# Moving the weight halves and the moving operands by 16 to 96 bytes in SBUF, in a two-block transformer kernel

## The chip, the cores and the metric

The kernel runs on one core of a Trainium2 chip. The metric is the device time of one execution in microseconds: the median of several runs.

## What is computed

Two different transformer blocks are applied in turn to 256 tokens of width 2048 in float32: a retention and state-space mixer with a gated output and a feed-forward layer, then a mixer of attention, gated linear attention and a short convolution, and a second feed-forward layer. Cut to the products that take the time:

```python
# first block
proj = h @ w_in                                        # 2048 -> 13312 columns
y_ret = (silu(g_ret) * ret) @ w_ret_out
glu_a, glu_b = split(y_ssm @ w_s5_glu, 2)
y = (sigmoid(gate_r) * y_ret + sigmoid(gate_s) * y_s5) @ w_out
a, b = split(h @ w_ffn_in, 2); y = (silu(a) * b) @ w_ffn_out     # width 5632
# second block: its own w_in, three branch products, w_out, gate/up/down of 5632
```

All of it is dense float32 work on weights that are read once, about 700 MB in all.

## The kernel before

The output features lie on partitions: each output block of 128 features is a sum over input blocks of 128 (the index `k`), with a 128 x 128 weight tile as the stationary operand and the 256 tokens as the moving one.

**The split.** A float32 product is made of several products in the reduced type `float32r`. Each weight block of 16 tiles (1 MB) comes by DMA into one of four ring slots, `ring_raw`. ScalarE writes its rounded half to `ring_hi` (`split_hi`, L1017), and VectorE writes the remainder, raw minus rounded, to `ring_lo` (`split_lo`, L1477). `ring_raw` and `ring_lo` of a slot share one address, so this subtraction is in place. The activations are held split too: in `h_split`, `ffn_split`, `mixed_split` and the like, each `k` has 256 rounded columns and behind them 256 remainder columns.

**The products.** `products()` makes one tile's work. In the first block's mixer (`p.thirds`) it is three matmuls of 256 columns: rounded weights by rounded activations (L635), rounded weights by remainders (L636), remainder weights by rounded activations (L637). Everywhere else it is two: rounded weights by all 512 columns (L638), then remainder weights by 256 (L639). Each matmul has its own weight load, which the profile shows as PEld. The order of all work is written out by hand; SyncE's queue issues the weight DMAs as slots come free, ScalarE rounds, VectorE subtracts, TensorE waits for `lo_done` of a block and then runs its 16 tiles.

**The addresses.** All operands lie at fixed SBUF addresses. The allocator is a stack: a tensor starts behind the one before it, rounded up to 32 bytes, and what is opened in a closed `ExitStack` gives its place to the next. The first ring slot starts at byte 1152 of each partition, which is 9 x 128. Worked out from the declared sizes, these are the starts as remainders of 128 bytes. Every step inside a tensor that a matmul makes (512 bytes from tile to tile, 1024 and 2048 in the moving operand) is a multiple of 128, so the remainder holds for each matmul of that tensor.

| operand | role | before | after |
|---|---|---|---|
| `ring_hi` (all slots) | weights, rounded half | 0 | 0 |
| `ring_raw`, `ring_lo` | weights, raw and remainder half | 0 | 16 |
| `h_split`, `ffn1_split`, `ffn2_split` | moving | 32 | 32 |
| `o_att_split`, `o_gla_split`, `y_conv_split` | moving | 32 | 32 |
| `ret_split`, `merged_split` | moving | 64 | 32 |
| `y_ssm_split` | moving | 64 | 96 |
| `mixed_split` | moving | 0 | 96 |

Of the kernel before, what the change touches and what calls it, by code (L numbers as in the profile page):

```python
# [23 lines left out]
F32R = mybir.dt.float32r  # L24
# [5 lines left out]
P = 128  # L30
T = 256
D = 2048
KT = D // P
# [18 lines left out]
PI_IN = 3.1415925  # L52
ROUND = 1.5 * 2.0 ** 23
SLOTS = 4
W, ADA = "w", "ada"


class Phase:
# [7 lines left out]
    def __init__(self, iters, blocks, outs, summed=False, beside=1):  # L66
# [5 lines left out]
        self.asides = len(blocks) - len(self.tiles)  # L72
        assert len(self.tiles) % SLOTS == 0 and outs % 2 == 0
        self.offsets = [sum(n for _, n in blocks[:j]) * P * P for j in range(len(blocks))]
# [8 lines left out]
    def uses(self, g, m):  # L83

        return g * (len(self.tiles) // SLOTS) + (self.first_block // SLOTS + m // SLOTS + 1)

# [116 lines left out]
def program(nc, dram, out):  # L203
    stored, ph = schedule(), stages()
    with ExitStack() as ctx:
        def sb(stack, name, shape, dt=F32):
            return stack.enter_context(nc.sbuf_tensor(name, shape, dt))

        def sem(name):
            return ctx.enter_context(nc.semaphore(name))  # L210


        raw, hi, lo = [], [], []
        for s in range(SLOTS):
            with ExitStack() as shared:
                raw.append(sb(shared, f"ring_raw{s}", [P, KT, P]))
            lo.append(sb(ctx, f"ring_lo{s}", [P, KT, P], F32R))
            hi.append(sb(ctx, f"ring_hi{s}", [P, KT, P], F32R))
        with ExitStack() as shared:
            s5_tab = [sb(shared, f"s5_tab{i}", [P, 2, 2, T]) for i in range(2)]  # L220
# [25 lines left out]
        with ExitStack() as block1:  # L246
            c_act = sb(block1, "c_act", [P, D])
            with ExitStack() as mixer:
                log_g = sb(mixer, "log_g_sb", [P, HEADS])
                wv = [[], []]  # L250
                with ExitStack() as shared:
                    wv[0] = [sb(shared, f"wv_a{n}", [P, 4, 4, P]) for n in range(4)]
# [4 lines left out]
                with ExitStack() as shared:  # L257
                    first_gates = sb(shared, "first_gates", [P, 4, 2 * T])
                merged = sb(mixer, "merged_split", [P, KT, 2 * T], F32R)
                with ExitStack() as shared:  # L260
                    sb(shared, "y_ssm_first", [P, HALF // 2, 2 * T])
                    aside_y = sb(shared, "aside_y", [P, D])
# [56 lines left out]
        with ExitStack() as block2:  # L319
            with ExitStack() as mixer:  # L320
# [27 lines left out]
                    a_end = sb(early, "a_end", [P, GLA_HEADS, T])  # L348
                t0 = sb(mixer, "merge0", [P, KT, T])
                conv_w = sb(mixer, "conv_w_sb", [P, HALF, 3])  # L350
                with ExitStack() as early:
                    gq = sb(early, "gq", [P, T])
                    gk = sb(early, "gk", [P, T])
                    gv_t = sb(early, "gv_t", [P, 2, T])
                    gr_t = sb(early, "gr_t", [P, 2, T])
                    gr_act = sb(early, "gr_act", [P, 2, T])
                    q_in = [sb(early, f"q_in{i}", [P, T]) for i in range(2)]
                    k_in = sb(early, "k_in", [P, T])
                    k_dec = sb(early, "k_dec", [P, T])
                    gv_n = sb(early, "gv_n", [P, 2, T])  # L360
                    k_dec_n = sb(early, "k_dec_n", [P, 3, P])
                    intra = sb(early, "intra", [P, 2, P])
                    state = [sb(early, f"state{i}", [P, T]) for i in range(3)]
                    go = sb(early, "go", [P, 2, T])
                    go_sq = sb(early, "go_sq", [P, 2, T])
                    go_std = sb(early, "go_std", [P, T])
                    go_rstd = sb(early, "go_rstd", [P, T])
                    att_q = [sb(early, f"att_q{i}", [P, T]) for i in range(2)]
                    att_k = [sb(early, f"att_k{i}", [P, T]) for i in range(2)]
                    att_v = [sb(early, f"att_v{i}", [P, T]) for i in range(2)]  # L370
# [27 lines left out]

        raw_in = [sem(f"raw_in{s}") for s in range(SLOTS)]
        wv_in = [[sem(f"wv_in{b}{part}") for part in range(2)] for b in range(2)]  # L400
        x_first = [sem(f"x_first{n}") for n in range(2)]
        c_set, hf_done, v_step, v_done, v_evac = (sem(n) for n in ("c_set", "hf_done", "v_step", "v_done", "v_evac"))
        late_row_in, late_row_free = sem("late_row_in"), sem("late_row_free")
        slot_free = [sem(f"slot_free{s}") for s in range(SLOTS)]
        hi_done, lo_done = sem("hi_done"), sem("lo_done")
# [103 lines left out]
        def _(sp):  # L509
# [40 lines left out]
            def weight(p, g, m, src):  # L550

                sp.wait_ge(slot_free[m % SLOTS], p.uses(g, m) - 1)
                sp.dma_start(raw[m % SLOTS][:].rearrange("p k c -> p (k c)"), src).then_inc(raw_in[m % SLOTS], 16)
# [1842 lines left out]
```

## Time and profile before

| | |
|---|---|
| median of 3 runs | 3386.57 us (3383.78 to 3386.83) |
| the profiled execution's own time | 3381.64 us |
| its span, first to last instruction | 3379.9 us |
| TensorE matmul busy | 3307.3 us, 98% of the span, 20368 matmuls |
| VectorE busy | 2324.5 us, 69% |
| ScalarE busy | 1452.4 us, 43% |
| mean granted TensorE clock | 0.992 |
| DMA | 706 MB, 209 GB/s |

How to read it: an engine's busy time is the union of its instructions; matmuls are pipelined, so one matmul's duration reaches over the start of the next, and what a matmul costs in a stream is the distance from its start to the start of the next. Durations and these distances move together here: the profile gives the 256-column matmul of `merged_split` 276 ns and starts the next about 113 ns later; it gives that of `ffn_split` 282 ns and the next starts about 118 ns later.

### The profile page before, as it was taken

How to read it: one execution, taken by the hardware profiler on the slowest of the kernel's cores; microseconds unless marked ns; L12 is line 12 of the kernel's file. 1: busy time of each engine (PE TensorE's matmuls, PEld its weight loads, DVE VectorE, ACT ScalarE, POOL GpSimd, SP SyncE). 2: the span in 40 equal slices, each digit the busy share in tenths (PEclk: the TensorE clock that was granted, in tenths of full speed). 3: DMA queues.
4: the chain of work that ended last, by engine and by line, in shares of the span. 5: the costliest groups of instructions: out<-in, count | busy, mean ns of one | idle time of the engine just before them, and what ended most of it. 6: DMA issues, size and time to landing. Idle time of an engine off the chain costs nothing.

```text
span 3379.9 us, 51972 instructions
## 1 busy us (share of the span) xinstructions
PE 3307.3 (98%) x20368; PEld 2937.2 (87%) x20368; DVE 2324.5 (69%) x2503; ACT 1452.4 (43%) x1464; POOL 435.2 (13%) x309
## 2 busy tenths in 40 slices
PE   6999999999899999999899999999999999999998
PEld 3599999999788888888788888888888888888887
DVE  6789979877766666666666667566767766666554
ACT  2256664444443444433454443444344444344332
POOL 1047668500100000000000000000003000000000
PEclk9999999999999999999999999999999999999999
DMA  9885456678545555577534444555555555555554
GB/s 378 349 328 180 180 202 237 251 292 311 198 175 188 192 191 186 195 268 254 198 137 169 167 162 178 193 183 186 192 186 196 188 188 186 189 192 186 185 191 149
DMA packets 119746, 706.34 MB, mean 209 GB/s; under 512 B 13776, under 2 KB 28752, under 8 KB 41312
## 3 DMA queue, kind: packets, MB, share of 16 engines
q1 hardware_dynamic: 109280, 695.96, 56.2%
q10 hardware_dynamic: 10368, 9.02, 0.8%
q8 instruction: 68, 1.11, 0.1%
q14 instruction: 30, 0.25, 0.0%
HBM read 702.83 MB, written 2.10 MB: 209 GB/s over the span
## 4 chain that ended last, share of the span: by engine, by line
PE 90%; DVE 5%; ACT 1%; DMA 1%; SPq 1%; issue 1%; DVEq 0%; ACTq 0%
PE acc L638 45%; PE acc L639 24%; PE acc L635 6%; PE acc L636 6%; PE acc L637 6%; DVE ring_raw L1499 1%; DVE ring_lo L1477 1%; DMA ring_raw<-w_ada 1%; SPq L542 1%; PE p_y L705 1%; PE p_norm L687 1%; PE p_z L715 1%; ACT ring_hi L1017 0%; DMA ring_raw<-w_out 0%; DVE rstd L1524 0%
## 5 line engine op out<-in xcount | busy, mean ns | idle before, releaser
L638 PE MATMUL acc<-h_split,ring_hi 128*128 128x512 f32 x4736 | 1655.9, 392 | 9.5 <-DVE h_split L1539 4.5
L1477 DVE TENSOR_TENSOR ring_lo<-ring_raw,ring_hi 128x2048 fp32r<-128x2048 f32 (+2 forms) x560 | 1265.1, 2260 | 550.2 <-ACT ring_hi L1017 549.1
L639 PE MATMUL acc<-h_split,ring_lo 128*128 128x256 f32 x4736 | 1337.6, 282 | 0.0
L1017 ACT ACTIVATE ring_hi<-ring_raw 128x2048 fp32r<-128x2048 f32 (+2 forms) x560 | 1040.0, 1862 | 458.6 <-DMA ring_raw<-w_down 150.4
L638 PEld LDWEIGHTS acc<-h_split,ring_hi 128*128 128x128 f32 x4736 | 891.9, 188 | 197.6 <-issue 10.0
L639 PEld LDWEIGHTS acc<-h_split,ring_lo 128*128 128x128 f32 x4736 | 897.9, 190 | 0.4
L638 PE MATMUL acc<-ffn_split,ring_hi 128*128 128x512 f32 x1408 | 488.2, 390 | 0.0
L2146 POOL TENSOR_TENSOR sq_sum<-sq_sum,tile 128x256 f32<-128x256 f32 x60 | 79.6, 1326 | 2561.6 <-ACT tile L1043 2561.6
L639 PE MATMUL acc<-ffn_split,ring_lo 128*128 128x256 f32 x1408 | 397.1, 282 | 0.0
L635 PE MATMUL acc<-h_split,ring_hi 128*128 128x256 f32 x1152 | 329.2, 286 | 0.3 <-ACT val_a L1030 0.2
L637 PE MATMUL acc<-h_split,ring_lo 128*128 128x256 f32 x1152 | 321.6, 279 | 0.0
L636 PE MATMUL acc<-h_split,ring_hi 128*128 128x256 f32 x1152 | 321.6, 279 | 0.0
L638 PEld LDWEIGHTS acc<-ffn_split,ring_hi 128*128 128x128 f32 x1408 | 264.4, 188 | 55.4
L639 PEld LDWEIGHTS acc<-ffn_split,ring_lo 128*128 128x128 f32 x1408 | 266.1, 189 | 0.0
L635 PEld LDWEIGHTS acc<-h_split,ring_hi 128*128 128x128 f32 x1152 | 216.6, 188 | 1.8 <-issue 0.6
L636 PEld LDWEIGHTS acc<-h_split,ring_hi 128*128 128x128 f32 x1152 | 216.6, 188 | 1.1 <-issue 0.2
L637 PEld LDWEIGHTS acc<-h_split,ring_lo 128*128 128x128 f32 x1152 | 216.6, 188 | 0.0
L1310 ACT ACTIVATE ffn_split<-ffn_a 128x256 f32 (+1 forms) x88 | 36.8, 418 | 361.5 <-DVE ffn_a L1903 361.5
L1492 DVE TENSOR_REDUCE ffn_b<-acc 128x256 f32<-128x512 f32 x88 | 60.8, 691 | 143.2 <-PE acc L639 143.2
L1043 ACT ACTIVATE tile<-x_res 128x256 f32 (+1 forms) x80 | 33.1, 417 | 152.1 <-DVE x_res L2127 85.2
L1308 ACT ACTIVATE ffn_t<-ffn_a 128x256 f32<-128x256 f32 x88 | 36.7, 417 | 129.3 <-DVE ffn_a L1899 119.2
L2204 POOL TENSOR_TENSOR s_x<-s_w,s_tab 128x512 f32<-128x512 f32 x32 | 86.6, 2707 | 29.9 <-DVE s_w L1688 29.8
(381 smaller groups left out, 3936.5 us busy)
## 6 DMA issues: line engine op xcount, KB each, us to landing
ring_raw<-w_ff SPq DMA_DIRECT2D x88, 1024.0 KB, 4.8
ring_raw<-w_down SPq DMA_DIRECT2D x64, 1024.0 KB, 4.8
ring_raw<-w_ffb SPq DMA_DIRECT2D x56, 1024.0 KB, 4.8
ring_raw<-w_mix SPq DMA_DIRECT2D x48, 1024.0 KB, 4.8
ring_raw<-w_ada SPq DMA_DIRECT2D x32, 1024.0 KB, 11.9
ring_raw<-w_heads SPq DMA_DIRECT2D x32, 1024.0 KB, 4.8
ring_raw<-w_ret SPq DMA_DIRECT2D x32, 1024.0 KB, 5.2
ring_raw<-w_glu SPq DMA_DIRECT2D x32, 1024.0 KB, 4.9
```

The lines of the kernel that those rows point to most:

```text
L635: mm(dst[:, 0:T], hi[s][:, t, :], moving[:, k, 0:T], start=start, stop=False)
L636: mm(dst[:, 0:T], hi[s][:, t, :], moving[:, k, T:], start=False, stop=False)
L637: return mm(dst[:, 0:T], lo[s][:, t, :], moving[:, k, 0:T], start=False, stop=stop)
L638: mm(dst[:], hi[s][:, t, :], moving[:, k, :], start=start, stop=False, skip_group_check=True)
L639: return mm(dst[:, T:], lo[s][:, t, :], moving[:, k, 0:T], start=False, stop=stop, skip_group_check=True)
L1017: run(hi[s][:, 0:n, :], raw[s][:, 0:n, :], COPY).then_inc(hi_done, 1)
L1308: run(t[i % 2][:], a[i % 2][:], ACT.Tanh, scale=0.5).then_inc(f_tanh, 1)
L1310: run(dst[:, 4 * g + (first + i), 0:T], a[i % 2][:], COPY, scale=0.5).then_inc(f_hi, 1)
L1477: tt(lo[s][:, 0:n, :], raw[s][:, 0:n, :], hi[s][:, 0:n, :], SUB).then_inc(lo_done, 1)
L1492: v.tensor_reduce(dst, acc[o % 2][:].rearrange("p (c t) -> p t c", c=2), AX_X, ADD).then_inc(sum_done, 1)
L2146: tt(sq_sum[:], sq_sum[:], tile[b][:], ALU.add).then_inc(sq_used, 1)
L2204: tt(xs[:], w[:], sin, ALU.mult)
```

## The change

The allocations alone are changed; no instruction, order or size of a transfer is. Each `ring_raw` and `ring_lo` gets 128 bytes more per partition, and its 16 tiles are taken from the fifth float on, that is 16 bytes past the tensor's start. Three unused pads (96, 64 and 96 bytes) are put ahead of `ret_split` and `merged_split`, of `y_ssm_split` and of `mixed_split`. The table above has what comes out for the operands of the large matmuls. Everything behind the ring moves up by 512 bytes, and some of the mixer's small tensors, the state-space matrices among them, change their remainder by 32.

```diff
+LO_AT = slice(4, 4 + KT * P)
...
             with ExitStack() as shared:
-                raw.append(sb(shared, f"ring_raw{s}", [P, KT, P]))
-            lo.append(sb(ctx, f"ring_lo{s}", [P, KT, P], F32R))
+                raw.append(sb(shared, f"ring_raw{s}", [P, KT * P + 32])[:, LO_AT].rearrange("p (k c) -> p k c", k=KT))
+            lo.append(sb(ctx, f"ring_lo{s}", [P, KT * P + 32], F32R)[:, LO_AT].rearrange("p (k c) -> p k c", k=KT))
             hi.append(sb(ctx, f"ring_hi{s}", [P, KT, P], F32R))
...
                 log_g = sb(mixer, "log_g_sb", [P, HEADS])
+                sb(mixer, "ret_step", [P, 24])
...
                 merged = sb(mixer, "merged_split", [P, KT, 2 * T], F32R)
+                sb(mixer, "y_step", [P, 16])
...
                 conv_w = sb(mixer, "conv_w_sb", [P, HALF, 3])
+                sb(mixer, "mixed_step", [P, 24])
```

## Rows read from the trace of the kernel before

**Rows 1.** The page: busy time of each engine (share of the span) and instructions.

```profile
PE 3307.3 (98%) x20368; PEld 2937.2 (87%) x20368; DVE 2324.5 (69%) x2503; ACT 1452.4 (43%) x1464; POOL 435.2 (13%) x309
```

**Rows 2.** The page: the chain that ended last, by engine and line.

```profile
PE 90%; DVE 5%; ACT 1%; DMA 1%; SPq 1%; issue 1%; DVEq 0%; ACTq 0%
PE acc L638 45%; PE acc L639 24%; PE acc L635 6%; PE acc L636 6%; PE acc L637 6%; DVE ring_raw L1499 1%; DVE ring_lo L1477 1%; DMA ring_raw<-w_ada 1%; SPq L542 1%; PE p_y L705 1%; PE p_norm L687 1%; PE p_z L715 1%; ACT ring_hi L1017 0%; DMA ring_raw<-w_out 0%; DVE rstd L1524 0%
```

**Rows 3.** Groups of instructions: shape, count, busy us, mean ns, idle before.

```profile
L638 PE MATMUL acc<-h_split,ring_hi 128*128 128x512 f32 x4736 | 1655.9, 392 | 9.5 <-DVE h_split L1539 4.5 <-DVE h_split L1537 4.4 <-DVE ffn_a L1492 0.4
...
L1477 DVE TENSOR_TENSOR ring_lo<-ring_raw,ring_hi 128x2048 fp32r<-128x2048 f32 (+2 forms) x560 | 1265.1, 2260 | 550.2 <-ACT ring_hi L1017 549.1
L1017 ACT ACTIVATE ring_hi<-ring_raw 128x2048 fp32r<-128x2048 f32 (+2 forms) x560 | 1040.0, 1862 | 458.6 <-DMA ring_raw<-w_down 150.4 <-DMA ring_raw<-w_mix 64.7 <-DMA ring_raw<-w_ret 49.8
...
L638 PE MATMUL acc<-mixed_split,ring_hi 128*128 128x512 f32 x256 | 89.9, 393 | 0.0
```

**Rows 4.** Matmuls by moving tile: duration ns min/median/max, first and last start.

```profile
L638 PE MATMUL acc<-ffn_split,ring_hi x1408: 390/390/390, 1417.9 to 3365.1; 128*128 128x512 f32 x176
L639 PE MATMUL acc<-ffn_split,ring_lo x1408: 282/282/282, 1418.1 to 3365.3; 128*128 128x256 f32 x176
...
L638 PE MATMUL acc<-y_conv_split,ring_hi x128: 390/390/390, 2248.6 to 2542.2; 128*128 128x512 f32 x128
...
L638 PE MATMUL acc<-mixed_split,ring_hi x256: 387/396/400, 2542.5 to 2632.0; 128*128 128x512 f32 x128
L639 PE MATMUL acc<-mixed_split,ring_lo x256: 278/283/285, 2542.8 to 2632.3; 128*128 128x256 f32 x128
...
L636 PE MATMUL acc<-h_split,ring_hi x1152: 277/280/284, 154.6 to 808.7; 128*128 128x256 f32 x192
...
L636 PE MATMUL acc<-ret_split,ring_hi x256: 276/280/283, 450.7 to 633.6; 128*128 128x256 f32 x128
...
L636 PE MATMUL acc<-y_ssm_split,ring_hi x256: 276/276/283, 658.1 to 814.1; 128*128 128x256 f32 x128
...
L636 PE MATMUL acc<-merged_split,ring_hi x256: 276/276/276, 814.4 to 902.8; 128*128 128x256 f32 x128
```

**Rows 5.** Timeline of TensorE, start us and us: first and last of nine pairs.

```profile
1500.08 0.39 PE L638 MATMUL acc<-ffn_split,ring_hi 128*128 128x512 f32 x1
1500.31 0.28 PE L639 MATMUL acc<-ffn_split,ring_lo 128*128 128x256 f32 x1
...
1503.20 0.39 PE L638 MATMUL acc<-ffn_split,ring_hi 128*128 128x512 f32 x1
```

**Rows 6.** Timeline, `mixed_split`: a short pair, and the start six pairs later.

```profile
2580.08 0.39 PE L638 MATMUL acc<-mixed_split,ring_hi 128*128 128x512 f32 x1
2580.30 0.28 PE L639 MATMUL acc<-mixed_split,ring_lo 128*128 128x256 f32 x1
...
2582.18 0.39 PE L638 MATMUL acc<-mixed_split,ring_hi 128*128 128x512 f32 x1
```

**Rows 7.** Timeline, three-matmul stages: `merged_split` (17 on), then `h_split` (14 on).

```profile
860.04 0.28 PE L637 MATMUL acc<-merged_split,ring_lo 128*128 128x256 f32 x1
...
861.97 0.28 PE L636 MATMUL acc<-merged_split,ring_hi 128*128 128x256 f32 x1
...
199.81 0.28 PE L636 MATMUL acc<-h_split,ring_hi 128*128 128x256 f32 x1
...
201.45 0.28 PE L635 MATMUL acc<-h_split,ring_hi 128*128 128x256 f32 x1
```

**Rows 8.** Windows: busy us of each engine (instructions), PEclk, DMA share, GB/s.

```profile
0.00:100.00 100.00, 73.89 (x166) 33.56 (x167) 66.08 (x113) 23.35 (x45) 16.82 (x21) 0.93 0.99 384
...
200.00:300.00 100.00, 99.64 (x793) 97.56 (x793) 95.60 (x122) 58.88 (x62) 72.62 (x47) 1.00 0.63 231
...
1000.00:1100.00 100.00, 100.00 (x579) 88.63 (x578) 63.73 (x63) 41.45 (x37) 0.00 (x0) 1.00 0.53 190
```

**Rows 9.** DMA issues: tile, count, KB each, median us to landing.

```profile
ring_raw<-w_ff SPq DMA_DIRECT2D x88, 1024.0 KB, 4.8
...
aside_z<-w_heads SPq DMA_DIRECT2D x9, 1024.0 KB, 4.9
```

**Rows 10.** Plain float32 matmuls of 256 columns: duration ns min/median/max.

```profile
L705 PE MATMUL p_y<-s_x,s_c_sb x128: 377/378/382, 230.1 to 652.2; 128*128 128x256 f32 x128
```

## The prediction

> **What bounds the kernel.** I read the page first: TensorE is busy in 98% of the span and no other engine above 69% [rows 1]. The chain of the work that ended last says the same by line: 90% of it is TensorE, and the five matmul lines of `products()` carry 87% [rows 2]. So time goes one for one with the distance between matmul starts, as long as TensorE stays fed. The windows show that: from 1000 us on a stretch of 100 us has TensorE busy for all of it and VectorE for 64 [rows 8].
>
> Then I asked what a matmul costs in the stream. In the second feed-forward product nine pairs (L638 and L639) take from 1500.08 to 1503.20 us, 3.12 us, or 346.7 ns a pair: 228 ns for the one of 512 columns and 118 for the one of 256 [rows 5]. Their durations differ by 390 - 282 = 108 ns for 256 columns [rows 4], 0.42 ns a column, which is the cycle of the clock's upper level of 2.4 GHz (the granted clock is 1.00 from 1000 to 1100 us too [rows 8]). 768 columns are then 320 ns, and 26.7 ns of each pair are something else.
>
> The reader is to see next that this rest is not one fixed price. The same instructions, with the same shapes and with the same ring, have other durations by moving tensor [rows 4], and the tensors differ in their start address. With `merged_split` (64 past a 128-byte line) every matmul of 256 columns has 276 ns; with `ffn_split` (32 past) its neighbour in a pair has 282; with `h_split` in the three-matmul stages (32 past) 277 to 284, median 280. With `mixed_split` (0 past) the 512-column one swings between 387 and 400, where all of 32 past have 390 without spread. In starts: 17 matmuls of `merged_split` in 1.93 us are 113.5 ns each, 14 of `h_split` in 1.64 us are 117.1 [rows 7]; `mixed_split` takes 2.10 us for six pairs, 350 ns a pair [rows 6]. A duration less 163 ns is the distance to the next start in all of these. But the address is not all of it: `ret_split`, at 64 like `merged_split`, goes from 276 to 283 with median 280, and `y_ssm_split`, at 64 too, has a median of 276 with a tail to 283 [rows 4]. One pair of addresses can thus run in more than one pattern.
>
> **The change part by part.** No instruction and no wait is added or removed. There are 4736 + 1408 + 3 x 128 = 6528 pairs (the three tensors of 128 have one pattern, that of `y_conv_split`) whose moving operand stays at 32 and whose remainder weights go from 0 to 16; 256 pairs of `mixed_split`, from 0 to 96; and 1152 + 3 x 256 = 1920 groups of three, of which 1152 (`h_split`) keep their moving address [rows 3, 4].
>
> *The pairs.* The weight load of the remainder half starts with the 512-column matmul and is read beside it; that of the next rounded half is read beside the 256-column matmul. The change alters the first combination of addresses directly and the second by where in its pattern it begins. No row has weights at 16, so the cost is bounded by what the rows show at other remainders. The lowest are 387 ns for 512 columns (2580.08 to 2580.30 is one such [rows 6]) and 276 for 256 columns [rows 4]. Against 390 and 282 that is 3 + 6 = 9 ns a pair, 6528 x 9 = 58.8 us. Lower still would be the fixed part of `merged_split`, 113.5 - 106.7 = 6.8 ns, on both: 220.1 + 113.5 = 333.6 ns a pair, 13.1 less than now, 85.5 us. Above stands the pair of `mixed_split`, 393 + 283 in the means against 390 + 282, 4 ns more, 26 us. I take 58.8: it is the lowest that rows show for both shapes, and an address that serves both weight halves is more likely near what `merged_split` has than at a new low. The reason for the sign is that 26.7 ns of a pair are now lost to something that the rows show to depend on addresses, and that the present combination loses more in its 256-column member (11.6 ns over 106.7) than `merged_split` does in each of three.
>
> *`mixed_split`.* 393 and 283 in the mean to 387 and 276: 13 ns x 256 = 3.3 us. In the worst case it stays.
>
> *The groups of three.* `h_split` from 117.1 to 113.5 ns: 3.6 x 3456 = 12.4 us. `ret_split` from a median of 280 to 276, 4 x 768 = 3.1. `y_ssm_split` and `merged_split` have nothing to give. From 200 to 300 us, though, VectorE is busy for 95.6 of 100 [rows 8]: there a faster TensorE waits for `lo_done` instead. I keep half of 15.5, 7.8 us. In the bad case `y_ssm_split` and `merged_split`, 1536 matmuls, lose 4 ns each, 6.1 us.
>
> *Who feeds the pairs.* A block of 16 pairs takes 5.55 us now and 5.40 then. Its subtraction takes 2.26 us on VectorE and its rounding 1.86 on ScalarE [rows 3], 63.7 and 41.5 of 100 busy with all else [rows 8], and its transfer 4.8 us to landing, of four in flight [rows 9]. If the 16 bytes made one of them 5% slower, cover would hide it. Below nothing I see no reason for a gain there.
>
> *The DMA writes.* All rows of 8 KB now begin 16 bytes past a line. A tensor at 64 past lands as one at 0 past: 4.9 us for `aside_z`, 4.8 for `ring_raw` [rows 9]. 16 past no row shows. It matters where DMA sets the pace, in the first 150 us, with a DMA share of 0.99 in the first 100 [rows 8]. One further line of 128 bytes per row would be 1/64, 2.3 us of these 150; the other bound is 0. I take 0, since the 64-past row differs by 0.1 us in 4.8 at most, and keep 2.3 for the range.
>
> *The small products.* L705 and its kind (plain float32) have 378 ns, 215 to the next start, for 256 columns at half the rate, 213 ns [rows 10]: 2 ns of rest. There is next to nothing in them to win.
>
> Sum: 58.8 + 3.3 + 7.8 = 69.9 us. The profiled execution's own time is 3381.64 (span 3379.9 and 1.7 around it); less 69.9 it is 3311.7. The median of the runs is 4.9 above that execution, so I forecast 3316.6 us on the scale of the median.
>
> **A page that speaks against it.** The rows say that the distance of like matmuls depends on the moving tensor's place. The Trainium skill, "TensorE: Matmul & The Clock Gate", section "Step-by-step: what each phase is for", says that TensorE reads moving and stationary operands through two SBUF ports of their own, so that loading the next weights takes no read bandwidth from the running matmul. By that rule the addresses of the weights would be free, and the change would give nothing, 3387. This case's trace does not agree in full, since 276 and 282 ns [rows 4] have the same weights at the same address, but it doesn't show that it is the weights' address that counts.
>
> **The rivals.**
> - *Only a part is given back*, chance 0.22. The remainder load is read beside the 512-column matmul alone. If just that one goes from 390 to 387, it is 3 x 6528 = 19.6 us; if just the 256-column one, 6 x 6528 = 39.2. With or without the 11 us of the rest, 3336 to 3367, middle 3352. For it: only one of two weight addresses moves in 6528 pairs. Against: the two are locked in one pattern, 390 and 282 without spread, and so change together.
> - *Nothing changes*, chance 0.12: the weights' address doesn't matter, only the moving one's. Then the pairs stay, `mixed_split` gains up to 3, and `merged_split` and `y_ssm_split` lose up to 6: 3384 to 3390. For it: rows differ only by moving tensor, all with the ring at 0. Against: `ret_split` and `merged_split` differ at one moving address, so something beside it takes part.
> - *Slower*, chance 0.21: at 16, the remainder weights fall into a pattern as `mixed_split`'s. It is one mechanism, the pair of weight load and 512-column matmul, at 4 ns more: 26 us, and 6 more where `merged_split` leaves its good address, 3413 to 3419. It decides as soon as a pair takes over 348 ns (1 ns x 6784 = 6.8 us is the measurement's bound). For it: the only other combination seen in pairs is worse than the present one on average. Against: within it stand pairs of 387, lower than the present.
> - *Deeper*, chance 0.05: pairs at 333.6 ns or below, 3281 or lower (85.5, 16.4 x 256 = 4.2 for `mixed_split` and all 15.5 of the groups of three are 105.2 us). If the rest of each matmul were 2 ns as in the plain products [rows 10], a pair would be 324 ns, 154 us less over all pairs: 3222 with the groups' 11.
>
> **How the numbers follow.** The forecast, pairs between 333 and 340 ns (3281 to 3325), has 0.40. Faster by over 0.2% are the forecast, the partial and the deeper case: 0.67. Within 0.2%, about what a measurement of this kernel can tell from no change: 0.12. Slower: 0.21. The likeliest case's own range is 3281 to 3325. For 8 in 10 it reaches over the partial and the unchanged case and takes in the 2.3 us of DMA, to 3396, which leaves out most of the slower case, and below to 3272, which leaves out most of the deeper one.
>
> **What would show it.** In the profile after: `ffn_split` at L638 with 387 or less and at L639 with 276; 9 pairs in 3.04 us in place of 3.12; about 593 matmuls per 100 us for 579; `merged_split` still at 276 at its new address; L1477 and L1017 with 2260 and 1862 ns; `ring_raw` landing in 4.8 us. Wrong would be the forecast if 390 and 282 stand as they are, if a spread as `mixed_split`'s appears in all pairs, or if TensorE begins to wait for `ring_lo`.

## The result and the profile after

The changed kernel takes 3400.58 us (median of 5, 3399.07 to 3402.09); the kernel before 3386.57 in the same comparison. The ratio is 1.0044, 95% interval 1.0032 to 1.0057: slower by 0.4%, where the prediction named 3316.6 and a faster time. The ratios here, though not the medians, leave out two single executions of later versions, one of 8797.62 us in twelve (80/16) and one of 11486.07 in ten (48/112), which nothing here explains. The changed kernel's profiled execution took 3399.39 us, with a span of 3397.6. Lines are four further down than before: L642 and L643 are the pair, L639 to L641 the group of three.

The page's first part and the shares of the chain:

```profile
PE 3326.8 (98%) x20368; PEld 2933.9 (86%) x20368; DVE 2323.0 (68%) x2503; ACT 1452.1 (43%) x1464; POOL 429.4 (13%) x309
...
PE 93%; DVE 4%; ACT 1%; DMA 1%; SPq 1%; issue 0%; DVEq 0%; ACTq 0%
PE acc L642 46%; PE acc L643 23%; PE acc L639 6%; PE acc L640 6%; PE acc L641 6%; DVE ring_raw L1503 1%; DMA ring_raw<-w_ada 1%; SPq L546 1%; PE p_z L719 1%; PE p_y L709 1%; DVE ring_lo L1481 1%; PE p_norm L691 0%; DVE rstd L1528 0%; ACT ring_hi L1021 0%; ACT tile L1047 0%
```

TensorE is busy for 3326.8 us in place of 3307.3 [rows 1], 19.5 more, with the same 20368 matmuls; VectorE and ScalarE have what they had. The feeders are untouched by the 16 bytes (groups of instructions: count, busy us, mean ns; then the DMA issues):

```profile
L1481 DVE TENSOR_TENSOR ring_lo<-ring_raw,ring_hi 128x2048 fp32r<-128x2048 f32 (+2 forms) x560 | 1263.4, 2257 | 557.9 <-ACT ring_hi L1021 556.8
L1021 ACT ACTIVATE ring_hi<-ring_raw 128x2048 fp32r<-128x2048 f32 (+2 forms) x560 | 1040.0, 1861 | 460.5 <-DMA ring_raw<-w_down 152.5 <-DMA ring_raw<-w_mix 66.3 <-DMA ring_raw<-w_ret 50.1
```

```profile
ring_raw<-w_ff SPq DMA_DIRECT2D x88, 1024.0 KB, 4.8
```

So the time is in the distances between matmuls. By moving tile, duration ns min/median/max:

```profile
L642 PE MATMUL acc<-ffn_split,ring_hi x1408: 389/393/403, 1426.6 to 3382.8; 128*128 128x512 f32 x176
L643 PE MATMUL acc<-ffn_split,ring_lo x1408: 277/280/284, 1426.8 to 3383.1; 128*128 128x256 f32 x176
...
L642 PE MATMUL acc<-mixed_split,ring_hi x256: 389/392/447, 2557.4 to 2646.5; 128*128 128x512 f32 x128
...
L640 PE MATMUL acc<-merged_split,ring_hi x256: 277/281/284, 818.6 to 909.0; 128*128 128x256 f32 x128
```

Before, `ffn_split` had 390 and 282 without any spread, and `merged_split` 276 [rows 4]. Now the pair wanders, and how is the clue. These are starts of L643 that lie 16 pairs, one ring slot's worth, apart (timeline of TensorE, first in a gate and up stage of the first block, then in the second block's):

```profile
1000.05 0.28 PE L643 MATMUL acc<-h_split,ring_lo 128*128 128x256 f32 x1
...
1005.66 0.28 PE L643 MATMUL acc<-h_split,ring_lo 128*128 128x256 f32 x1
...
1011.26 0.28 PE L643 MATMUL acc<-h_split,ring_lo 128*128 128x256 f32 x1
...
1016.81 0.28 PE L643 MATMUL acc<-h_split,ring_lo 128*128 128x256 f32 x1
...
1022.38 0.28 PE L643 MATMUL acc<-h_split,ring_lo 128*128 128x256 f32 x1
...
2800.18 0.28 PE L643 MATMUL acc<-h_split,ring_lo 128*128 128x256 f32 x1
...
2805.76 0.28 PE L643 MATMUL acc<-h_split,ring_lo 128*128 128x256 f32 x1
...
2811.30 0.28 PE L643 MATMUL acc<-h_split,ring_lo 128*128 128x256 f32 x1
```

In the first stretch it is 5.61, 5.60, 5.55 and 5.57 us, and then the same four again; worked out from the exact starts, 351.2, 349.9, 346.4 and 348.4 ns a pair. In the second it is 5.58 and 5.55 us, 348.8 and 346.6 ns a pair, and then these two again. Four is the number of slots, and two is after how many slots the addresses repeat within 256 bytes, as the experiments show. Before the change all four slots had 346.7. From 1000 to 1300 us there are 1721 matmuls where there were 1733, 349.0 ns a pair.

Summed over all distances from a matmul to the next, `h_split` has 11.4 us more than before, `ffn_split` 3.9, `merged_split` 2.2, `y_ssm_split` 2.2, the three tensors of 128 pairs 0.7; `mixed_split` has 0.4 less, `ret_split` 0.4 less, everything else 1.5 less. That is 18.1; the first matmul starts 0.4 us earlier, and the span has 17.7 more. The 11.4 us of `h_split` are two things: 8.1 in its pairs, and 3.4 in its groups of three, which go from 350.3 to 353.4 ns in the mean. All pairs whose moving operand stays where it was lose 12.6 us together, 1.9 ns each.

### The profile page after: what moved, and what is told of

It is laid out like the page before. It is cut to its first block, busy times and chain, and to the rows that moved or that the text cites. A ratio compares the mean times of both kernels' runs of the same rounds, so it can differ in the third digit from the quotient of the medians.

```text
span 3397.6 us, 51972 instructions
## 1 busy us (share of the span) xinstructions
PE 3326.8 (98%) x20368; PEld 2933.9 (86%) x20368; DVE 2323.0 (68%) x2503; ACT 1452.1 (43%) x1464; POOL 429.4 (13%) x309
## 4 chain that ended last, share of the span: by engine, by line
PE 93%; DVE 4%; ACT 1%; DMA 1%; SPq 1%; issue 0%; DVEq 0%; ACTq 0%
PE acc L642 46%; PE acc L643 23%; PE acc L639 6%; PE acc L640 6%; PE acc L641 6%; DVE ring_raw L1503 1%; DMA ring_raw<-w_ada 1%; SPq L546 1%; PE p_z L719 1%; PE p_y L709 1%; DVE ring_lo L1481 1%; PE p_norm L691 0%; DVE rstd L1528 0%; ACT ring_hi L1021 0%; ACT tile L1047 0%
## 5 line engine op out<-in xcount | busy, mean ns | idle before, releaser
L642 PE MATMUL acc<-h_split,ring_hi 128*128 128x512 f32 x4736 | 1665.4, 396 | 9.4 <-DVE h_split L1543 4.5
L1481 DVE TENSOR_TENSOR ring_lo<-ring_raw,ring_hi 128x2048 fp32r<-128x2048 f32 (+2 forms) x560 | 1263.4, 2257 | 557.9 <-ACT ring_hi L1021 556.8
L643 PE MATMUL acc<-h_split,ring_lo 128*128 128x256 f32 x4736 | 1327.0, 280 | 0.0
L1021 ACT ACTIVATE ring_hi<-ring_raw 128x2048 fp32r<-128x2048 f32 (+2 forms) x560 | 1040.0, 1861 | 460.5 <-DMA ring_raw<-w_down 152.5
L642 PEld LDWEIGHTS acc<-h_split,ring_hi 128*128 128x128 f32 x4736 | 894.1, 189 | 215.1 <-issue 10.2
L643 PEld LDWEIGHTS acc<-h_split,ring_lo 128*128 128x128 f32 x4736 | 894.5, 189 | 0.4
L642 PE MATMUL acc<-ffn_split,ring_hi 128*128 128x512 f32 x1408 | 492.1, 394 | 0.0
L643 PE MATMUL acc<-ffn_split,ring_lo 128*128 128x256 f32 x1408 | 394.2, 280 | 0.0
L639 PE MATMUL acc<-h_split,ring_hi 128*128 128x256 f32 x1152 | 330.6, 287 | 0.3
L641 PE MATMUL acc<-h_split,ring_lo 128*128 128x256 f32 x1152 | 322.7, 280 | 0.0
L642 PEld LDWEIGHTS acc<-ffn_split,ring_hi 128*128 128x128 f32 x1408 | 264.6, 188 | 61.4
L643 PEld LDWEIGHTS acc<-ffn_split,ring_lo 128*128 128x128 f32 x1408 | 265.4, 189 | 0.0
L639 PEld LDWEIGHTS acc<-h_split,ring_hi 128*128 128x128 f32 x1152 | 216.9, 188 | 1.7 <-issue 0.6
L641 PEld LDWEIGHTS acc<-h_split,ring_lo 128*128 128x128 f32 x1152 | 217.1, 188 | 0.0
```

The lines of the kernel that those rows point to most:

```text
L639: mm(dst[:, 0:T], hi[s][:, t, :], moving[:, k, 0:T], start=start, stop=False)
L641: return mm(dst[:, 0:T], lo[s][:, t, :], moving[:, k, 0:T], start=False, stop=stop)
L642: mm(dst[:], hi[s][:, t, :], moving[:, k, :], start=start, stop=False, skip_group_check=True)
L643: return mm(dst[:, T:], lo[s][:, t, :], moving[:, k, 0:T], start=False, stop=stop, skip_group_check=True)
L1021: run(hi[s][:, 0:n, :], raw[s][:, 0:n, :], COPY).then_inc(hi_done, 1)
L1481: tt(lo[s][:, 0:n, :], raw[s][:, 0:n, :], hi[s][:, 0:n, :], SUB).then_inc(lo_done, 1)
```

## The experiments

Theory A was: the 16 bytes of the remainder halves spoil the pattern. Theory B: the ring tensors have grown by 128 bytes each, so that one slot is 16512 bytes from the next in place of 16384; if the chip's cycle of addresses is longer than 128 bytes, the slots are no longer alike. Theory C was that the traffic of other engines causes the lost time. A combination of addresses is written as remainder weights/moving operand, in bytes past the rounded weights within 256 bytes; 80/16 is one. Values in ns per pair or per group of three are worked out from the starts in the trace; a pair is one matmul of 512 columns and one of 256.

**Only the slots' distance.** The change's ring with `LO_AT` from 0, no pads:

```diff
+LO_AT = slice(0, KT * P)
-                raw.append(sb(shared, f"ring_raw{s}", [P, KT, P]))
+                raw.append(sb(shared, f"ring_raw{s}", [P, KT * P + 32])[:, LO_AT]...)
...  (ring_lo the same)
```

> Ring slots get the 128 bytes more, but raw and remainder halves stay on the 128-byte line, and there are no pads: only the distance of the slots in memory changes, 16512 bytes for 16384. Theory A (the 16 bytes cost the time): as before, 3387 within 5 us, pairs of ffn_split at 390 and 282 without spread. Theory B (the slots' distance costs it): pairs change from slot to slot, 390 is spread, and the time moves by more than 5 us.

Measured: 3402.98 us, ratio 1.0056 (1.0039 to 1.0073). The remainder halves stand on the 128-byte line and the loss is there in full. But the edit changes two things at once. The slots differ in the moving operand's distance (160 in one, 32 in the next), and in all of them the remainder halves stand 128 bytes further from the rounded ones. No whole kernel takes these apart; the sweep below has 350.0 ns for 128/160 and 346.7 for 128/32. By moving tile:

```profile
L639 PE MATMUL acc<-ffn_split,ring_hi x1408: 391/394/400, 1427.4 to 3386.8; 128*128 128x512 f32 x176
```

**The ring's part of the change, no pads.** The diff of the change without its three `sb(mixer, ...)` lines.

> The ring's part of the change (16 bytes and 128 more per tensor) without the three pads. Theory A and B alike: the large pairs are as in the changed kernel, so about 3400 less what the pads cost: merged_split and y_ssm_split keep 64 bytes past the line. If the pads are what made the groups of three slower (4 ns x 1536 = 6 us), this one has 3394; if not, 3400.

Measured: 3401.88 us, 1.0055 (1.0038 to 1.0072). The pads are not what made it slow.

**The 16 bytes without the other distance.** The tensors grow by 256 bytes:

```diff
+LO_AT = slice(4, 4 + KT * P)
+                raw.append(sb(shared, f"ring_raw{s}", [P, KT * P + 64])[:, LO_AT]...)
...  (ring_lo the same)
```

> The 16 bytes of the change, but the tensors grow by 256 bytes in place of 128, so that all four slots are alike within 256 bytes; no pads. Theory B (the slots' distance did the harm, not the 16 bytes): the sweep has 346.7 ns for remainder weights 16 and moving 32 past the rounded ones, so 3386 within 6 us and one pair time in all slots. Theory A (the 16 bytes harm): 3395 or more.

Measured: 3389.79 us, 1.0017 (1.0007 to 1.0026), with 1733 matmuls from 1000 to 1300 us and 346.7 ns a pair in all slots. The 16 bytes cost the pairs nothing. The 0.17% is in the groups of three: those of `merged_split` go from 340.0 to 353.3 ns, those of `y_ssm_split` from 344.2 to 353.1, those of `h_split` from 350.3 to 352.5. By moving tile:

```profile
L637 PE MATMUL acc<-merged_split,ring_hi x256: 277/278/283, 820.5 to 911.2; 128*128 128x256 f32 x128
```

**The pads alone.** Only the three `sb(mixer, ...)` lines.

> The three pads alone, the ring as before. The pads move mixed_split from 128 to 224 past the rounded weights within 256 bytes (the sweep: 351.1 and 353.3 ns a pair, +0.6 us over 256 pairs), ret_split and merged_split from 64 to 160, y_ssm_split from 64 to 224: against now 340 to 353 ns a group the sweep has 356.0 and 355.0. Expected is 3 to 10 us slower than before, 3389 to 3396; if the pads do nothing, 3386.

Measured: 3387.21 us, 1.0010 (1.0000 to 1.0019): 0 to 0.2% slower, 2.5 us in the medians, just below the 3 to 10 that were expected.

**Address sweeps.** A kernel in which TensorE alone streams pairs, or groups of three, from chosen addresses; the rest of the computation is left out. Its core:

```python
for h, l, m in COMBOS:
    for n in range(STEPS):
        wh = hi[:, h // 4 + t * P:h // 4 + t * P + P]      # rounded weights at h bytes
        wl = lo[:, l // 4 + t * P:l // 4 + t * P + P]      # remainder weights at l
        at = m // 4 + t * 2 * T                            # moving operand at m
        mm(acc[:], wh, mv[:, at:at + 2 * T], ...)
        mm(acc[:, T:], wl, mv[:, at:at + T], ...)
```

> Leaves out all of the reference's computation (it copies x to the output) and streams pairs of matmuls, 512 and 256 columns, 24 pairs for each of 16 x 20 combinations of the remainder weights' and the moving operand's start, the rounded weights at 0 of a 512-byte line, all other engines idle. Theory A, only the remainder of 128 bytes counts: combinations that differ by 128 or 256 bytes have the same ns per pair; remainder weights at 0 with moving at 32 give 346.7 as in the kernel before. Theory B, the cycle of addresses is longer than 128 bytes, so that the four slots, which now stand 128 bytes apart in it, are four different cases: 0 and 128 differ by ns. Theory C, the other engines' traffic causes the lost time: all combinations have one and the same time, below 346.7.

> The same sweep with groups of three matmuls of 256 columns, 16 groups for each combination; it too leaves out all of the reference's computation. Theory A: 113.3 ns per matmul with both weights at 0 and moving at 64, 116.7 with moving at 32, and the same 128 bytes further. Theory B: other values 128 bytes further. Theory C: one value everywhere.

Some cells of the sweep of pairs, the rounded weights at 0 (ns per pair, the last 12 of 24):

```
remainder \ moving    0     32     64     96    128    160    256    288    320
      0             353.3  346.7  348.9  350.0  351.1  346.7  353.3  346.7  353.3
     64             346.7  353.3  340.0  346.7  346.7  353.3  346.7  348.9  340.0
    128             346.7  346.7  346.7  350.0  352.9  350.0  350.0  346.7  346.6
    256             353.3  346.7  348.9  350.0  351.1  346.7  353.3  346.7  353.3
    320             346.7  353.3  340.0  346.7  346.7  353.3  346.7  348.9  340.0
```

Moving the remainder weights by 256 bytes leaves 99 of 100 cells as they are (99 of 100 for groups of three), by 128 bytes only 57 of 160. For the remainder weights the cycle is 256 bytes. Moving the moving operand by 256 leaves 102 of 128, by 128 only 50 of 192: 256 is much nearer to a cycle for it than 128, but it is not shown to be one. Of the 26 cells that change, 18 are combinations that have one value from both starts in the full grid below, so a second pattern that a stream can fall into, or a longer cycle of the moving operand, are both open. No sweep moves the rounded weights alone. With nothing else running, remainder weights at 0 and moving at 32 give the kernel's own pattern, and at 128 that of `mixed_split`, member by member (by tile of the sweep; `aa` is 0, `ac` 32, `ai` 128, `ae` 64):

```profile
L66 PE MATMUL at_aa_aa_ac<-moving,w_hi x24: 390/390/396, 33.8 to 41.7; 128*128 128x512 f32 x24
L67 PE MATMUL at_aa_aa_ac<-moving,w_lo x24: 279/282/282, 34.0 to 42.0; 128*128 128x256 f32 x24
...
L66 PE MATMUL at_aa_aa_ai<-moving,w_hi x24: 387/396/402, 84.2 to 92.3; 128*128 128x512 f32 x24
...
L66 PE MATMUL at_aa_ae_ae<-moving,w_hi x24: 389/389/393, 721.7 to 729.5; 128*128 128x512 f32 x24
L67 PE MATMUL at_aa_ae_ae<-moving,w_lo x24: 276/276/278, 721.9 to 729.7; 128*128 128x256 f32 x24
```

390 and 282, and 387/396, are the figures of [rows 4]. That refutes theory C, and theory A in its form with 128 bytes.

**The full grid, twice.** All 256 combinations in steps of 16, each behind one matmul of another length (ns per pair, the last 8 of 16), and then some of them with all three operands moved together.

> Leaves out the reference's computation like the first sweep. Every combination of remainder weights and moving operand in steps of 16 bytes over 256, twice, each behind one matmul of another length, and then 128 combinations with the rounded weights at 16, 64, 128 and 208 of 256. Theory B2, only the distances between the three operands within 256 bytes count: the third part repeats the first at equal distances, and the second repeats the first. Theory B3, the state in which a stream begins counts too: some combinations have two values, in the first and the second part, while a few (remainder weights and moving both 64 past the rounded ones, 340.0 in six of six cases of the first sweep) keep one. Theory B4, absolute addresses count: the third part differs from the first for most combinations.

Times go from 340.0 to 363.4 ns, mean 349.3. In 200 of 256 combinations both starts give one value; in 56 they don't, so a stream can settle in more than one pattern. Five combinations have 340.0 from both starts: 32/144, 48/112, 80/16, 208/64 and 208/112 (remainder weights/moving operand past the rounded weights). With the rounded weights at 64 or 128 the single-valued cells repeat in 17 and 15 of 21, at 16 or 208 in 7 and 6 of 21. I passed over that second finding and built two versions of the kernel on distances alone.

**Two versions of the whole kernel at such distances.** Rounded halves 16 bytes into their tensors, slots 16640 bytes apart, pads for the moving operands:

```diff
+HI_AT = slice(4, 4 + KT * P)
-            hi.append(sb(ctx, f"ring_hi{s}", [P, KT, P], F32R))
+            hi.append(sb(ctx, f"ring_hi{s}", [P, KT * P + 24], F32R)[:, HI_AT]...)   # 80/16; raw and lo + 40
+        sb(ctx, "h_step", [P, 40])
+                sb(mixer, "ret_step", [P, 16])
+                sb(mixer, "mixed_step", [P, 40])
...  (48/112: raw and lo + 48, hi + 16, h_step 8, mixed_step 40, no ret_step)
```

> The whole kernel, with remainder weights 80 and the moving operands of all pairs 16 past the rounded weights within 256 bytes, the same in all four slots. The theory (only the three operands' distances within 256 bytes set the time of a matmul in the stream): the sweeps have 340.0 ns in three of three cases, so 6528 pairs x 6.7 = 43.5 us less, mixed_split 2.8 less, the groups of three of h_split at 353.1 for 350, 3.6 us more, merged_split and y_ssm_split (now 112 past) 5 more: 3347, within 10. The rival, that other engines' traffic or the starts of the blocks throw the stream out of the good pattern: pairs between 343 and 350, and 3365 to 3400.

> The same with remainder weights 48 and moving operands 112 past the rounded weights, the other combination that the sweeps have at 340.0 in three of three. The theory: groups of three of h_split at 354.7 ns, 5.4 us more, else as the one before: 3349 within 10. The rival: 3365 to 3400.

Measured: 3387.90 us, 1.0010 (1.0001 to 1.0019), and 3393.28, 1.0023 (1.0014 to 1.0033). Both missed: the pairs have 346.7 ns, the first with members of 392 and 279, the second with 394 and 278, where the sweeps had 340.0, with 389 and 276 for 80/16 and 388 and 275 for 48/112.

**Groups of three, the full grid.**

> Leaves out the reference's computation. The full sweep in steps of 16 bytes for groups of three matmuls of 256 columns, twice. The theory of distances within 256 bytes and of more than one pattern for some of them: a few combinations have 340.0 ns a group in both parts, many have two values, and those of the first sweep of groups come out again. If instead groups of three have one value for each combination, the spread between merged_split and ret_split needs another cause.

Six combinations have 340.0 in both parts and many have two values: 210 of 256 have one. Remainder weights 0 and moving 64, which is `merged_split` before, had 353.4 in both parts here, and 340 (276 a member) in the kernel.

**What held the two versions back?** One kernel with eight segments.

> Leaves out the reference's computation. Six combinations of remainder weights and moving operand (0 and 32, 16 and 32, 48 and 112, 80 and 16, 64 and 64, 208 and 64 past the rounded weights), 64 pairs each, in eight segments: alone; with the moving operand 90 KB up; with the weights far up; in a hardware loop with two banks; beside VectorE subtractions; beside ScalarE copies; beside 1 MB transfers; beside all three. The full kernels had 346.7 ns for 48 and 112 and for 80 and 16, the sweeps 340.0. Theory D, distance in memory beyond 256 bytes counts: the segment with the moving operand or the weights far up has 346.7 for them. Theory E, the loop or the change of banks counts: only the loop's segment has it. Theory F, the traffic of another engine moves the stream into its other pattern: 340.0 in the quiet segments and 346.7 beside one of the three, which names the engine.

Theories D, E and F all fell. 80/16 has 340.0 in every segment, with 19.7 of 20 us of VectorE or ScalarE beside it or 216 GB/s of transfers. Two windows (each begins in 80/16 and ends in 64/64, which has 340.0 too), and the tile alone (`near`) and beside all three (`byall`):

```profile
783.00:803.00 20.00, 20.00 (x120) 17.67 (x119) 0.00 (x0) 19.68 (x11) 0.00 (x0) 1.00 0.00 1
...
1050.00:1070.00 20.00, 20.00 (x120) 17.67 (x119) 19.73 (x9) 19.68 (x11) 0.00 (x0) 1.00 0.63 215
```

```profile
L90 PE MATMUL near_af_ab<-moving,w_hi x64: 387/389/399, 99.3 to 120.8; 128*128 128x512 f32 x64
```

```profile
L90 PE MATMUL byall_af_ab<-moving_far,w_hi x64: 388/389/399, 1034.5 to 1056.0; 128*128 128x512 f32 x64
```

48/112 had 356.7 in all quiet segments and 340.0 in the sweeps: again two patterns of one combination.

**The place of all three.** Eight combinations of distances, six of them in the table, the rounded weights at 0, 16, ... 128, three starts.

> Leaves out the reference's computation. Eight pairs of distances, each with the rounded weights at 0, 16, ... 128 past a line of 256 bytes, from three starts, 32 pairs each. Theory G, beside the distances the place of the three operands within 64 bytes counts (in the sweep the third part at 64 and 128 repeated the first, at 16 and 208 it did not, and these two agreed): values repeat when all three operands are moved by 64 bytes and not when by 16; the distances 80 and 16 with the rounded weights at 48 have 346.7 with members of 229 and 117, 48 and 112 with them at 80 has 346.7 with 232 and 115, as in the full kernels. Theory H, only the distances count and the full kernels were held in another pattern by something else: 340.0 for 80 and 16 at every place.

Values against the place of the rounded weights, counted over 15 streams (multiples of 32) and 12 streams (16 more than one), rounded ns:

```
remainder/moving   on a multiple of 32         16 past one
   0/32            347 in 15                   353 in 10, 347 in 2
  48/112           340 in 12, 357 in 3         347 in 12
  80/16            340 in 14, 353 in 1         347 in 12
  64/64            340 in 11, 350 in 4         350 in 12
 208/64            351 in 13, 340 in 2         340 in 12
 208/112           340 in 13, 353 in 2         351 in 7, 353 in 5
```

So the place within 32 bytes counts, not within the 64 of theory G. In the two versions the rounded weights stood at 48 and 80, 16 past a multiple of 32; the sweep has for these places what they had, with the same members (rounded weights at 48 with 80/16, then at 208/64 with them at 0 and at 16):

```profile
L67 PE MATMUL at_ad_ai_ae<-moving,w_hi x32: 392/392/437, 1332.5 to 1343.3; 128*128 128x512 f32 x32
L68 PE MATMUL at_ad_ai_ae<-moving,w_lo x32: 277/279/279, 1332.8 to 1343.6; 128*128 128x256 f32 x32
...
L67 PE MATMUL at_aa_an_ae<-moving,w_hi x32: 393/394/450, 1835.2 to 1846.2; 128*128 128x512 f32 x32
...
L67 PE MATMUL at_ab_ao_af<-moving,w_hi x32: 388/388/429, 1869.3 to 1879.9; 128*128 128x512 f32 x32
```

**Two versions with the rounded weights on a multiple of 32**, chosen before that sweep was read. `LO_AT` begins at float 52 or 16, the tensors grow by 64 floats, `h_step` is of 8 floats, `ret_step` of 48 or 8, `mixed_step` of 40:

> The full kernel with the rounded weights at 128, remainder weights 208 and moving operands of the pairs 64 past them, thus at places within 64 bytes that the sweeps had, and with 340.0 in ten of ten cases; the operands of the groups of three other than h_split 32 past. Theory G: 340.0 ns a pair, 43.5 us less, mixed_split 2.8 less, groups of three 7 more: 3347 within 10. Theory H: 346.7 a pair and 3385 to 3395.

> The same with remainder weights and moving operands 64 past, the other operands of three at 128 past. The sweeps have 340.0 in eight of nine cases and 350.0 in one. Theory G: 340.0 and 3348 if every stream falls into the better pattern, 350.0 and 3413 if into the other, and between them if both occur. Theory H: as for the one before.

Measured: 3413.98 us, 1.0090 (1.0076 to 1.0105), and 3359.76, 0.9935 (0.9913 to 0.9958). The first was expected fast and is the slowest of all: ten streams had 340.0 there, and the sweep by places, not yet read, has 351 in 13 of 15, in all three with the rounded weights at 0, where the sweeps before it had theirs, so the value hangs on something beside the addresses that no run names; the kernel has 350.9 to 351.4. The second beats both kernels, with runs from 3348.68 to 3378.11: in the trace most of its `h_split` pairs and all of `ffn_split` stand at 340.0, and the branch products and `mixed_split` of the second block at 350.0, the two values of 64/64. By moving tile:

```profile
L642 PE MATMUL acc<-ffn_split,ring_hi x1408: 389/389/389, 1414.3 to 3341.2; 128*128 128x512 f32 x176
...
L642 PE MATMUL acc<-mixed_split,ring_hi x256: 395/395/395, 2532.8 to 2622.0; 128*128 128x512 f32 x128
```

**A version with one pattern.** 208/64 with the rounded weights at 176 of 256, 16 past a multiple of 32; all moving operands of pairs taken 16 bytes into their tensors:

```diff
+        def stepped(stack, name, k, dt=F32):
+            t = sb(stack, name, [P, k * 2 * T + 8], dt)
+            return t[:, 4:4 + k * 2 * T].rearrange("p (k c) -> p k c", k=k)
...
+            hi.append(sb(ctx, f"ring_hi{s}", [P, KT * P + 56], F32R)[:, HI_AT]...)   # from float 4; raw and lo + 8
+        sb(ctx, "h_step", [P, 16])
+        h = stepped(ctx, "h_split", KT, F32R)
...  (normed, ffn1_split, ffn2_split, o_att and o_gla in one tensor, y_conv_split, mixed_split the same, with pads of 56, 56, 56, 56 and 32 floats)
```

> The full kernel at the distances 208 and 64 again, but with the rounded weights 16 past a multiple of 32 (176 of 256), the moving operands of all pairs at 240 and the remainder weights at 128. The sweep by places has 340.0 ns in 12 of 12 cases there, and 350.9 or 340.0 with the rounded weights on a multiple of 32, which was the version at 3414. Distances within 256 bytes and the place within 32 bytes fix the pair: 340.0 in every stretch, 6528 x 6.7 = 43.5 us less, mixed_split 2.8 less, groups of three unknown, between 20 less and 12 more: 3330 to 3355, and runs within 5 us of each other, for there is one pattern. If something else of the kernel counts: 346.7 or more, 3385 and above.

Measured: 3348.12 us, runs from 3347.82 to 3348.48, ratio 0.9896 (0.9879 to 0.9912): 1.0% faster than the kernel before and, from the two ratios, 1.5% than the changed one, and inside the window that was named. The pairs give back what was expected; the groups of three take back about 11 us of it (an estimate from the trace: 354.8 ns for 350.3 in `h_split`, 353.3 for 340.0 in `merged_split`, 353.5 for 344.2 in `y_ssm_split`). By moving tile, and ten pairs in 3.40 us:

```profile
L650 PE MATMUL acc<-ffn_split,ring_hi x1408: 388/388/389, 1417.1 to 3331.8; 128*128 128x512 f32 x176
L651 PE MATMUL acc<-ffn_split,ring_lo x1408: 275/275/275, 1417.3 to 3332.0; 128*128 128x256 f32 x176
```

```profile
1500.08 0.39 PE L650 MATMUL acc<-ffn_split,ring_hi 128*128 128x512 f32 x1
...
1503.48 0.39 PE L650 MATMUL acc<-ffn_split,ring_hi 128*128 128x512 f32 x1
```

**The groups of three, 16 bytes further.**

> Leaves out the reference's computation. The full sweep of groups of three with all three operands 16 bytes further. If the place within 32 bytes counts, the groups' times differ from those of the full sweep before in many cells; if distances alone count for groups of three, they repeat it.

Of the 170 combinations with one value in each of the two grids, 47 have the same in both. The place counts for them as well.

## Why the prediction was wrong

**What bounds the kernel: right.** Every version's time followed the distance of its matmuls; VectorE's busy time stayed between 2323 and 2329 us and ScalarE's between 1452 and 1457 in all of them.

**The step that failed is the term of the pairs**, 58.8 us of gain, and in it the choice "it is the lowest that rows show for both shapes". Its size and its sign were wrong: in `ffn_split` the trace has 393 and 280 ns in the median for 387 and 276, and the pairs lost 12.6 us. Three things stood behind the choice. First, all was reasoned in remainders of 128 bytes, as the title of the change has it. Within 256 bytes the change does something else: `ring_raw` and `ring_lo` are 128 bytes longer, so the remainder weights come to stand 144 bytes past the rounded ones, not 16, and the moving operand 160 past them in one slot and 32 in the next. The grid has 343.4 or 351.6 for 144/160 and 351.5 or 349.2 for 144/32. The 16 bytes that I weighed are worth nothing to a pair: 16/32 has 346.7. Second, the bounds were prices of other combinations, and the value taken was the lower end of them; a combination that is not in the trace is one draw from a table that reaches from 340.0 to 363.4 with a mean of 349.3, and the kernel before had a better draw than the mean. Third, 387 and 276 were the lowest durations of two different streams put together, 337.7 ns a pair; no stream of pairs in any sweep or version has less than 340.0, which comes as 389 and 276 or 388 and 275. In `mixed_split`, from which the 387 was taken, a pair cost 351.0 ns in the mean.

**The slower rival**, at 0.21, had the way and the kind of pattern (a spread like `mixed_split`'s, and `merged_split` leaving its good address), but not the cause: at 16 past, with the slots alike, the pairs keep 346.7; the pattern comes with the 128 bytes. Its size, 3413 to 3419, was too large: the pairs went to 348.4 ns in `h_split` and 349.4 in `ffn_split`, a loss of 12.6 us for its 26.

**`mixed_split`**: forecast 3.3 us of gain, measured 0.4. **The groups of three**: forecast 7.8 of gain with a bad case of 6.1 of loss; measured 7.4 of loss. `merged_split` and `y_ssm_split` lost 4.4 us, `h_split`'s groups 3.4 where a gain was forecast, and `ret_split` gained 0.4. This term's sign was wrong too. **DMA, VectorE and ScalarE at 16 bytes**: taken at 0, and so it is (2257 ns, 1861 ns, 4.8 us). **The small products**: nothing, as said.

**The unchanged rival and the page beside it.** That the weights' address does not matter is refuted by runs that move it alone: in the sweep, with the moving operand at 64, the pair has 348.9 ns with remainder weights at 0 and 340.0 with them at 64. The Trainium skill's "TensorE: Matmul & The Clock Gate", section "Step-by-step: what each phase is for", has the next load take no read bandwidth from the running matmul. That the weights' address would then be free does not hold here: with the moving operand at 208 the grid goes from 346.6 to 363.4 ns a pair by the remainder weights' address alone, and the measurement decides. Whether it is read bandwidth that is shared, no run shows. The Trainium skill's "TensorE: Matmul & The Clock Gate", section "Back-to-back issue gap", has 518 and 262 cycles for single matmuls of these lengths; at 2.4 GHz that is an estimate of 216 and 109 ns, 325 a pair. The lowest that any stream here reached is 340.0.

**What stays open.** No run shows why: the sweeps give a table, with a cycle of 256 bytes for the remainder weights, a dependence on the place within 32, and more than one pattern for at least a fifth of the combinations. What the two readers share, and what decides the pattern in which a stream settles, is not settled. Nor is the cycle of four slots in the changed kernel: within 256 bytes its slots 0 and 2 are alike, and so are 1 and 3, which fits the two values from 2800 us on but not the four from 1000 us on. The ring's part alone has the same addresses for these pairs within 256 bytes, and yet 349.1, 344.3, 351.2 and 351.2 ns from 1000 us on. `merged_split`'s 276 ns in the kernel before beside 353.4 a group in the grid is one such case, which no run here explains beyond that.

## What to carry to other kernels

Where TensorE runs matmuls back to back with a weight load for each, a changed tensor size in the ring can change the speed. Growing two tensors of each slot by 128 bytes cost 0.6% here (1.0056), with every operand's remainder of 128 bytes as it was. Work in remainders of 256 bytes and give every ring slot the same one, so that a stage runs one combination of addresses and not several. That alone makes nothing fast: with equal slots the versions here went from 3348 to 3414 us. Then look at the distances of rounded weights, remainder weights and moving operand to each other, and at spread in a matmul's duration by tile (390/390/390 against 389/393/403). And take such prices from a sweep that runs each combination from several starts and at its true place, for a value that came out of other starts, or 16 bytes away, misled three versions here.

## What the runs showed of the hardware that was not expected

- The distance of like matmuls in a stream depends on the SBUF addresses of three operands in steps of 16 bytes: 340.0 to 363.4 ns for the same pair. For the remainder weights it repeats after 256 bytes (99 of 100 cells); for the moving operand 102 of 128 cells do.
- The place within 32 bytes changes it too: 208/64 has 351 ns in 13 of 15 streams on a multiple of 32 and 340 in 12 of 12 when 16 past one.
- The same distances and the same place can hold two patterns, for hundreds of pairs: 64/64 had 340.0 in `ffn_split` (1408 pairs) and 350.0 in `mixed_split` (256 pairs) of one execution.
- Traffic of VectorE, ScalarE and DMA beside the stream, at 98% busy and 216 GB/s, left 80/16 at 340.0 in a kernel of streams alone.
